# Spreading the four 256-slot experts among the twelve 128-slot ones in a two-layer mixture-of-experts stage

## What is computed

```python
# per layer, x is 256 x 1024; 16 experts in 4 groups of 4, D_EXPERT = 256
g_sel = argmax(group_score)            # each token picks ONE group of 4 experts
gates = ...                            # and 2 experts in that group, weights sum to 1
h = silu(einsum('nd,edf->enf', xt, w_gate)) * einsum('nd,edf->enf', xt, w_up)
h = h * gates.T[:, :, None]
y = einsum('enf,efd->nd', h, w_down)
x = layer_norm(ALPHA * x + y, ln2_g, ln2_b)
```

## Time and profile before

| | us |
|---|---|
| median of 3 runs (lowest, highest) | 1383.97 (1383.74, 1385.13) |
| the profiled execution: time | 1379.53 |
| the profiled execution: span from first to last instruction | 1377.7 |
| mean granted TensorE clock in it | 0.917 |
| PE busy / DVE busy / ACT busy | 1192.6 (87%) / 782.8 (57%) / 586.9 (43%) |
| chain that ended last: PE, DVE, DMA, ACT | 66%, 13%, 9%, 7% |

### The profile page before, as it was taken

The page is one execution under the profiler, slowest core; times in us unless marked ns, Lnnn a source line. Parts: engine busy times, 40 slices in busy tenths (PEclk is TensorE's granted clock), DMA queues, the critical chain, the costliest instruction groups (busy, mean ns, idle before and its releaser), DMA issues.

```text
span 1377.7 us, 17333 instructions
## 1 busy us (share of the span) xinstructions
PE 1192.6 (87%) x6958; PEld 1040.3 (76%) x6958; DVE 782.8 (57%) x946; ACT 586.9 (43%) x706; POOL 104.0 (8%) x151
## 2 busy tenths in 40 slices
PE   4999899997999989868859999887958858998885
PEld 4999899987999979747657876666936747886664
DVE  5344545775444455465355467766367454557775
ACT  3444445633333333344124456553334314446661
POOL 3000101000000002610000000000621000000000
PEclk9999999998999998857969999998975978999997
DMA  8644434562555553300134569882410006468990
GB/s 270 211 144 123 151 122 150 175 209 99 195 183 183 184 175 97 114 19 1 31 121 153 182 219 312 307 294 85 144 54 3 31 31 213 136 200 284 309 317 37
DMA packets 115077, 215.87 MB, mean 157 GB/s; under 512 B 9546, under 2 KB 79178, under 8 KB 115008
## 3 DMA queue, kind: packets, MB, share of 16 engines
q1 hardware_dynamic: 112432, 209.90, 46.2%
q0 software_dynamic: 1424, 4.59, 1.0%
q10 hardware_dynamic: 1152, 0.42, 0.1%
HBM read 213.80 MB, written 1.09 MB: 156 GB/s over the span
## 4 chain that ended last, share of the span: by engine, by line
PE 66%; DVE 13%; DMA 9%; ACT 7%; issue 3%; POOL 1%; SPq 1%; POOLq 0%; ACTq 0%; DVEq 0%
PE ps L735 15%; PE ps L737 15%; PE ps L736 14%; DMA raw<-in_w_up 6%; DVE wlo L1546 6%; ACT whi L1202 4%; PE ps L794 3%; PE ps L771 3%; PE ps L821 3%; PE ps L772 3%; PE ps L773 3%; DMA raw<-in_w_down 2%; PE ps L806 2%; PE ps L1079 1%; PE ps L1080 1%
## 5 line engine op out<-in xcount | busy, mean ns | idle before, releaser
L1546 DVE TENSOR_TENSOR wlo<-raw,whi 128x2048 fp32r<-128x2048 f32 (+1 forms) x199 | 445.9, 2243 | 323.5 <-ACT whi L1202 322.6
L1202 ACT ACTIVATE whi<-raw 128x2048 fp32r<-128x2048 f32 (+1 forms) x199 | 369.5, 1861 | 227.2 <-PE ps L737 112.5
L735 PE MATMUL ps<-act_hi,whi 128*128 128x256 f32 (+1 forms) x784 | 228.1, 291 | 11.0 <-DVE act_lo L1553 11.0
L736 PE MATMUL ps<-act_lo,whi 128*128 128x256 f32 (+1 forms) x784 | 226.0, 288 | 0.0
L737 PE MATMUL ps<-act_hi,wlo 128*128 128x256 f32 (+1 forms) x784 | 225.9, 288 | 0.0
L735 PEld LDWEIGHTS ps<-act_hi,whi 128*128 128x128 f32 (+1 forms) x784 | 152.2, 194 | 17.3 <-DVE act_lo L1553 12.6
L736 PEld LDWEIGHTS ps<-act_lo,whi 128*128 128x128 f32 (+1 forms) x784 | 152.1, 194 | 1.2
L737 PEld LDWEIGHTS ps<-act_hi,wlo 128*128 128x128 f32 (+1 forms) x784 | 152.0, 194 | 1.0
L735 PE MATMUL ps<-whi,moe_r 128*128 128x512 f32 x320 | 132.8, 415 | 18.2 <-DVE wlo L1546 17.9
L737 PE MATMUL ps<-whi,moe_r 128*128 128x512 f32 x320 | 128.6, 402 | 0.0
L736 PE MATMUL ps<-wlo,moe_r 128*128 128x512 f32 x320 | 128.2, 401 | 0.0
(11 more groups left out here) (258 smaller groups left out, 1945.8 us busy)
## 6 DMA issues: line engine op xcount, KB each, us to landing
raw<-in_w_in SPq DMA_DIRECT2D x45, 1024.0 KB, 5.5
raw<-in_w_down SPq DMA_DIRECT2D x43, 1024.0 KB, 5.0
raw<-in_w_gate SPq DMA_DIRECT2D x64, 512.0 KB, 4.4
raw<-in_w_up SPq DMA_DIRECT2D x64, 512.0 KB, 5.2
raw<-in_w_gu SPq DMA_DIRECT2D x22, 1024.0 KB, 5.1
raw<-in_w_out SPq DMA_DIRECT2D x12, 1024.0 KB, 4.9
raw<-in_p_b SPq DMA_DIRECT2D x2, 1024.0 KB, 5.2
raw<-in_p_c SPq DMA_DIRECT2D x2, 1024.0 KB, 5.3
```

The lines of the kernel that those rows point to most:

```text
L735: pe.matmul(o, ah, bh, start=first, stop=False)
L736: pe.matmul(o, ah, bl, start=False, stop=False)
L1202: act.activation(whi[:, c % 3, 0:n], raw[:, c % 3, 0:n], ACT.Copy).then_inc(hi_made, 1)
L1546: dve.tensor_tensor(wlo[:, c % 3, 0:n], raw[:, c % 3, 0:n], whi[:, c % 3, 0:n].bitcast(F32), ALU.subtract)\
```

## The change

Experts are now indexed by x, their place in an order `MOE_SEQ`: one two-unit expert, three one-unit ones, four times. A unit u is a pair (x, q). The parts:

1. SP, ACT, DVE and PE take the tiles as A(x), B(x), D(x-1) for every x.
2. `down` stands one expert behind its gate and up, after tile B of the next expert.
3. The transposes of a unit's product go into the gate half of the unit's own bank (`u % 2`) and not to bank 2. So a unit may only start when the hidden of the unit two before has been split (`bank_free`).
4. `turn_hidden` of the previous expert's last unit stands between the first and second six matmuls on tile A; the first unit of a two-unit expert is turned after its tile B.
5. The gather of q = 2, 3, 4 is moved ahead of the first expert, over banks 2, 4, 5, 6, 7; so is its ACT and DVE work, among the first splits.
6. The transposes of `put` are moved behind `down` of x = 13, their copies to ACT's program of x = 15. SP reads a group's position register when the group first occurs.
7. At the end both scatters of q 0 to 3 stand before the last `down`, whose output is split in two halves (`y_half`).

The core of the diff (DVE's program mirrors ACT's, SP's mirrors `moe_order`):

```diff
+MOE_SEQ = [0, 4, 5, 6, 1, 7, 8, 9, 2, 10, 11, 12, 3, 13, 14, 15]
+MOE_UNITS = [(x, q) for x, e in enumerate(MOE_SEQ) for q in ((0, 1) if e < 4 else (e // 4 + 1,))]
+    for x in range(N_EXP):
+        at["A", x] = len(at)
+        at["B", x] = len(at)
+        if x:
+            at["D", x - 1] = len(at)
     at["D", N_EXP - 1] = len(at)
+OUT_AFTER = [12, 12, 5, 10, 15]
+REST_BANK = [2, 4, 5, 6, 7, 2, 4, 5]
...
 # PE
-                for q in range(5):
-                    for t in range(TT):
-                        x = pe.transpose(ps[:, q // 2, q % 2 * 256 + t * P:q % 2 * 256 + (t + 1) * P],
-                                         put[:, t, q * P:(q + 1) * P].bitcast(F32), ident)
-                x.then_inc(putt_full, 1)
...
+                for k in range(KD):
+                    if k >= 1:
+                        pe.wait_ge(xg_l, l * 12 + k)
+                    gather(ps[:, REST_BANK[k], 0:384], k, 256, 640).then_inc(xg_full, 1)
+                def bank_free(u):
+                    if u >= 2:
+                        pe.wait_ge(m_lo2, l * N_UNIT + u - 1)
...
+                for x in range(N_EXP):
+                    u = UNIT_AT[x]
+                    tile_ready(moe_tile(l, "A", x))
+                    bank_free(u)
+                    gate_up("A", u, 0, 2)
+                    if x:
+                        turn_hidden(u - 1)
+                    r = gate_up("A", u, 2, 4)
+                    if MOE_SEQ[x] < 4:
+                        bank_free(u + 1)
+                        r = gate_up("A", u + 1, 0, 4)
+                    r.then_inc(tile_used, 1)
+                    tile_ready(moe_tile(l, "B", x))
+                    r = gate_up("B", u, 4, 8)
+                    if MOE_SEQ[x] < 4:
+                        r.then_inc(m_gu, 1)
+                        r = gate_up("B", u + 1, 4, 8)
+                    r.then_inc(tile_used, 1)
+                    if MOE_SEQ[x] < 4:
+                        turn_hidden(u)
+                    if x == 0:
+                        pe.wait_ge(gsl_sb, l + 1)
+                        pe.wait_ge(xg_l, l * 12 + 12)
+                    else:
+                        down(x - 1)
+                    if x == N_EXP - 2:
...                     # the ten transposes of put, then putt_full
+                for half in range(2):
+                    scatter(0, half, 0, 4)
+                turn_hidden(N_UNIT - 1)
+                for half in range(2):
+                    scatter(1, half, 0, 4)
                 down(N_EXP - 1)
+                for half in range(2):
+                    pe.wait_ge(y_lo, l * 6 + 5 + half)
+                    for t in range(TT):
+                        r = scatter(t, half, 4, 5)
...
 # ACT
                 split("A", 0)
+                for k in range(KD):
+                    gathered(4 + k, xg_hi[:, k, 256:640], ps[:, REST_BANK[k], 0:384])
                 split("B", 0)
                 split("A", 1)
+                for x in range(N_EXP):
+                    u, n = UNIT_AT[x], UNIT_AT[x + 1] - UNIT_AT[x]
+                    if 1 <= x < N_EXP - 1:
+                        split("A", x + 1)
+                    if x == N_EXP - 1:
+                        split("D", x)
+                    for i in range(n):
+                        silu(u + i)
+                    if x < N_EXP - 1:
+                        split("B", x + 1)
+                    if n == 2:
+                        hidden(u)
...                     # out_rows at x = 6, 11, 13; copies of put_t at x = 15
+                    hidden(u + n - 1)
+                    if x < N_EXP - 1:
+                        split("D", x)
+                out_rows(4, 2, 2)
```

More of the change, by code:

```diff
@@ L1117, in half_hidden @@
[L1117 to L1128, removed]
@@ L1130, in down @@
-                def down(e):
-                    n = moe_tile(l, "D", e)
+                    o = ps[:, u % 2, :].rearrange("p (a b) -> p a b", a=2)
+                    m = slice(q * P, (q + 1) * P)
+                    for k in range(k0, k1):
+                        r = three(o, xg_hi[:, k, m], xg_lo[:, k, m], wh[:, :, k % 4, :], wl[:, :, k % 4, :], k == 0, k == KD - 1)
+                    return r
+                def bank_free(u):
+                    if u >= 2:
+                        pe.wait_ge(m_lo2, l * N_UNIT + u - 1)
@@ L1140, in down @@
                             for c in range(2):
[L1141 to L1147, removed]
-                        for q in range(q0, q1):
-                            w = put_t[:, q, t * P:(t + 1) * P]
-                            for i, y in enumerate((xg_hi, xg_lo)):
-                                x = pe.matmul(ps[:, b + half, :].rearrange("p (k d) -> p k d", k=4), w,
-                                              y[:, 4 * half:4 * half + 4, q * P:(q + 1) * P],
-                                              start=q == 0 and i == 0, stop=q == 4 and i == 1)
-                    return x
@@ new lines, in down, with scatter @@
+                            if x == N_EXP - 1 and half == 0:
+                                r.then_inc(y_half, 1)
+                    r.then_inc(tile_used, 1)
+                def scatter(t, half, q0, q1):
+                    for q in range(q0, q1):
+                        w = put_t[:, q, t * P:(t + 1) * P]
+                        for i, y in enumerate((xg_hi, xg_lo)):
+                            r = pe.matmul(ps[:, 4 + 2 * t + half, :].rearrange("p (k d) -> p k d", k=4), w,
+                                          y[:, 4 * half:4 * half + 4, q * P:(q + 1) * P],
+                                          start=q == 0 and i == 0, stop=q == 4 and i == 1)
+                    return r
@@ L1534, in _ @@
-                silu(N_EXP - 1, 4)
-                hidden(N_EXP - 1)
-                out_rows(4, N_EXP - 1)
+                for x in range(N_EXP):
+                    u, n = UNIT_AT[x], UNIT_AT[x + 1] - UNIT_AT[x]
[9 more added lines that the diff above has]
+                        hidden(u)
+                    if x == 6:
+                        out_rows(2, 2)
+                    if x == 11:
+                        out_rows(3, 2)
+                    if x == 13:
+                        out_rows(0, 4)
+                        out_rows(1, 6)
+                    if x == N_EXP - 1:
+                        act.wait_ge(putt_full, l + 1)
+                        act.activation(put_t[:, 0:4, :], banks(4, 6).rearrange("p (q t) -> p q t", q=4), ACT.Copy)
+                        act.activation(put_t[:, 4, :], ps[:, 6, 0:S], ACT.Copy).then_inc(putt_sb, 1)
+                    hidden(u + n - 1)
+                    if x < N_EXP - 1:
+                        split("D", x)
@@ new lines, in out_rows @@
+                def out_rows(i, q, b, halves=1):
+                    m = slice(q * P, (q + 1) * P)
+                    for h2 in range(halves):
+                        k = slice(h2 * 4, h2 * 4 + 8 // halves)
+                        dve.wait_ge(y_hi, l * 6 + i + h2 + 1)
+                        dve.tensor_tensor(xg_lo[:, k, m], banks(b + h2, b + 2 // halves + h2).rearrange("p (k d) -> p k d", d=P),
+                                          xg_hi[:, k, m].bitcast(F32), ALU.subtract).then_inc(y_lo, 1)
@@ L1964, in layer @@
                     gathered(i, xg_hi[m], xg_lo[m], ps[:, 4 + i, :].rearrange("p (k s) -> p k s", k=2))
+                for k in range(3):
+                    rest(k)
+                split("A", 0)
                 dve.wait_ge(gsl_full, l + 1)
@@ L2011, in layer @@
+                out_rows(4, 4, 2, 2)
                 if not last:
```

299 lines of the change are left out of this document (105 added, 194 removed).

## The result

The changed kernel is slower: 1398.74 us (median of 18 runs, 1392.74 to 1403.01) against 1383.61 us for the kernel before beside it (18 runs), ratio 1.0116, 95% interval 1.0099 to 1.0133. A ratio leaves out the few runs that took over 1.5% longer than the same kernel's fastest, with a lower mean clock, so it can differ a little from the quotient of the two medians. Forecast were 1385.2 us and a range up to 1391.5. The profiled execution took 1397.25 us with a span of 1395.4, against 1379.53 and 1377.7.

A forecast was written before the change was run, and what follows sets the result against it. Loads bound one-unit experts before; hiding them was to be spent on two ACT/DVE chains. First layer +1.1 us and second +0.1 gave +1.2: median 1383.97 to 1385.2 us, range 1380 to 1391.5.

The forecast's parts named there:

- The two chains: Written order on ACT and DVE holds PE: 9.2 us per one-unit expert, 16.6 us per two-unit expert.
- the ring's wait: At the next two-unit expert, tile A lands 1.3 us after ACT is ready; PE waits 0.3 us a group.
- the clock: At x = 0, 4.8 us of idle lowers the granted clock: some 4.3 us at half speed, 1.5 us lost.
- Start: Moved gather takes 7.7 us, half covered by 3.5 us of idle; tile A of x = 0 at 729.6, against 726.4.
- A one-unit expert: `down(x-1)` waits for D(x-1), split behind `hidden(x-1)`: 9.2 us, where PE's own work is 8.5.
- Behind a two-unit expert: `hidden` stands behind the split of B(x+1): 16.6 us, PE stalled 2.3 us, or 4.8 us at x = 0.
- One group: Four experts, one two-unit and three one-unit: 47.4 us for a middle group, against 47.8 before.
- rival (a): Clock falls at every stall behind a two-unit expert: 1.5 us for each of six further stalls, 1394.2; chance 0.10.
- End: Transposes of `put` 1.2 us, then scatters and last `down` 10.4; `residual` 7.05 us later in layer one, 2.2 in layer two.
- Rival (c): Landings of 5.8 us make the third one-unit expert and next A wait, 0.8 to 1.1 us a group: 1391.2; chance 0.12.
- Rival (d): The two chains do not bind and PE sets the pace, 42.6 us a group: 1344.6; chance 0.05.
- all against me: Stalls, one-unit links, ring wait and clock at x = 0 all at their bad bounds: about +8 us.

The follow-up runs named there:

- after_short: The changed kernel with only a part of each weight tile loaded in the expert stage: 1388.9 us, ratio 1.0086 to the kernel before.
- d_first: The changed kernel with the split of D(x) ahead of `hidden` where a one-unit expert comes next, on ACT and DVE: 1384.91 us, ratio 1.0057.
- hid_first: The changed kernel with the first unit's hidden of a two-unit expert split ahead of B(x+1), on ACT and DVE: 1371.6 us, ratio 0.9942.
- fill_idle: The changed kernel with twenty matmuls without a use in PE's 4.8 us idle time at x = 0: 1394.07 us, ratio 1.0099.
- gather_late: The changed kernel with the gather of blocks 2 to 4 back behind tile B of the first expert: 1400.17 us, ratio 1.0161.

## Why the prediction was wrong, point by point

Forecast was +1.2 us for the profiled execution; it was +17.7. The two chains were right, in place and size. What failed is mainly the sum for one group: the ring's wait in it, put at 0.3 us, was 1.2, and the wait for the bank of the second unit in tile A, put at nothing without a reason, made the two-unit experts 5.0 us longer in all. These two are 10.6 of the 16.5 us; the clock, at the start and behind the stalls, is most of the rest. All the terms that mattered were off to the same side.

- *Start.* Forecast tile A of x = 0 at +17.9 us from the first gather matmul, measured 730.86 - 712.20 = 18.7. The idle time did go away, but the slow clock did not (0.57 in 722 to 726 us): the gather now ran through it. +0.8 a layer, 1.6 in all. My sentence that the slow stretch of before "is gone" was wrong, and its premise, that the 3.55 us of idle had made it, does not hold here: PE is busy without a break. What makes the clock fall behind `gsl` was not tested.
- *A one-unit expert*, 9.2 us: measured 9.25. *Behind a two-unit expert*, 16.6 (16.4 at x = 0), 4.8 and 2.3 us: measured 16.6 in after_short, 16.39, 4.81 and 2.07. d_first and hid_first show that these are the two chains named.
- *One group.* Here most was lost. The ring's 0.3 us a group was 1.2 on average: third one-unit experts took 10.2 to 10.8 us where I had 9.2 + 0.3, 5.6 us over six groups. I had followed the passes with the median landing of before, and a median does not hold where the loads are issued one on another: those on the path took 5.9 to 7.7 us. after_short settles that it is the loads.
- *The wait in the middle of tile A.* The front text lists `bank_free` for every unit, and my calculation has it for the first only. ACT and DVE make `hidden(x-1)` behind a weight tile that landed late, and the second unit of a two-unit expert waits for it, 0.5 to 1.0 us in four of six. These experts took 16.7 to 18.0 us instead of 16.6, about 5.0 us in all. With short loads they take 16.6 in the middle groups and 17.1 in the last, so late landings are most of the cause once more; the last group's 0.5 us is `out_rows` ahead of `hidden(11)`, which I had not priced either.
- *The clock.* At x = 0, 1.9 for 1.5 us: 0.8 over both layers. And rival (a) came true in half: behind three of six stalls of 2.07 us (periods of 12.97, 12.96 and 13.12 for 12.07), 0.9 to 1.1 us each instead of 1.5: 2.8 us. The Trainium skill's rule ("TensorE: Matmul & The Clock Gate", section "A second HAM failure mode: psum-queue depth-cycling") that I weighed there, a clock swinging with idle times between groups of matmuls, describes what happened better than my count of harmless short waits did; by the runs it acts on some of these stalls and not on others.
- *End.* Transposes of `put` 1.2 and the last part 10.4: measured 1.22 and 10.5. From the last `down` to `residual` 7.05 and 2.2: measured 6.9 and 2.2.

1.6 + 5.6 + 5.0 + 0.8 + 2.8 = 15.8 of the 16.5 us between forecast and result. Rival (c) had the ring's mechanism and, with (a)'s, the sign. I gave the two 0.22 and took them one at a time, but both act on the same tight group, and late landings bring the bank waits with them. A range that takes them together ends at 1385.2 + 9 + 6 = 1400.2. Nor did the range hold its own bounds: all against me, they add up to 1.8 (stalls) + 2.4 (links) + 4.8 (ring) + 1.6 (clock at x = 0) = 10.6 us and not "about +8", and it ended at +6.3. Rival (d), chains that don't bind, was false of this kernel, but names their worth: with both chains out the kernel runs at 0.9836 of before, 1361 us on the median of 1383.97, somewhat over half of the way to the 1344.6 of that rival; the ring has a part of the rest (0.5 to 2.3 us a group).

## What to carry to other kernels

When a change lays a transfer-bound stretch over a compute-bound one, first ask of each in-order queue what now stands between an instruction and the engine that waits for it: two small splits behind two large ones cost here all that the overlap was worth, and more. Judge the reordering only with those put right: between the spread and the plain order of the changed kernel there was no difference to be seen with the chains, and 2.4% without them. For a ring of buffers take the landing time of loads issued together, not the median of all, and add up the bad cases that share a cause.

## What the runs showed of the hardware

- A PE idle for 2.07 us, in the same place of the same code, was followed by a granted clock near 0.5 in some cases and by 1.00 in others: in the profiled executions behind 3 of 6 such stalls (changed kernel), 4 of 6 (fill_idle), 5 of 6 (after_short), 5 of 6 (gather_late), 1 of 6 (d_first). After 4.81 us it fell in every case. Each fall cost 0.9 to 1.6 us behind the short stall and 1.9 us behind the long one. What decides the short case stays open. It may be part of why runs of the changed kernel differ by 10 us; that was not tested.
- The clock also fell with PE busy: in the changed kernel PE has no idle time from 712.20 on, runs 20 matmuls of four columns from 720.08 to 722.23 us, and stands at 0.57 in 722 to 726 us; hid_first has 0.57 in the same stretch.
- The up halves of weight tiles took 5.2 us to land at the median of the kernel before. In the changed kernel the six on the chain that ended last took 5.9 to 7.7 us; around the first two of them, issued close behind others, the DMA engines moved 336 and 344 GB/s.
- A matmul of 128x512 follows its neighbour after 0.23 us at clock 1.00 (fill_idle: 749.13, 749.36, 749.60) and after 0.43 us at the lower level (changed kernel: 748.23, 748.66, 749.09).
